# Expert weights of a mixture-of-experts kernel: GpSimd issues the next expert's staged loads itself

## The reference

```python
logits = (xt @ w_router) + b_router            # 256 tokens, 32 experts
top_v, top_i = lax.top_k(logits, 4)
gates = jax.nn.softmax(top_v, axis=-1)
# for the rows xb of each expert e:
hdn = xb @ w_gate_up[e] + b_gate_up[e]         # 1024 x 2048 weights
y = clamped_swiglu(hdn) @ w_down[e] + b_down[e]  # 1024 x 1024 weights
out = out.at[tok].add(y * gate)
```

## Time and profile before

| | |
|---|---|
| median of 3 runs | 2048.03 us (2046.79 to 2048.07) |
| profiled execution | 2044.31 us |
| its span | 2042.5 us |
| granted TensorE clock, mean | 0.982 |
| TensorE busy | 1941.8 us (95%) |
| GpSimd busy | 580.8 us (28%) |
| experts, first block to last | about 221 to 1179 us of the span |

### The profile page before, as it was taken

One profiled execution on the slowest core, in us unless ns is written; L12 is line 12 of the kernel. 1 busy time (PEld: TensorE's weight loads), 2 busy tenths in 40 slices (PEclk: granted clock), 3 DMA queues, 4 the chain that ended last, 5 costly groups with the idle time before them and its releaser, 6 DMA issues.

```text
span 2042.5 us, 28146 instructions
## 1 busy us (share of the span) xinstructions
PE 1941.8 (95%) x10641; PEld 1197.4 (59%) x10642; DVE 897.4 (44%) x1387; ACT 719.5 (35%) x1182; POOL 580.8 (28%) x622
## 2 busy tenths in 40 slices
PE   5997899999999999999999989999999999999998
PEld 2975333333333333333333379788888898898887
DVE  4644321121222112211122166658787575576983
ACT  2544111111111111111111156655665456646662
POOL 3230344442432444344433304000232030001340
PEclk7998899999999999999999989999999999999999
DMA  9999799998997999899999955445455454554553
GB/s 345 299 367 370 311 422 422 422 422 367 404 423 313 423 422 422 356 420 422 422 422 422 417 185 199 130 159 188 159 188 206 151 199 132 166 198 133 186 194 116
DMA packets 186533, 608.81 MB, mean 298 GB/s; under 512 B 10459, under 2 KB 115055, under 8 KB 133489
## 3 DMA queue, kind: packets, MB, share of 16 engines
q1 hardware_dynamic: 180976, 585.14, 74.4%
q0 software_dynamic: 5152, 21.67, 3.0%
q10 hardware_dynamic: 328, 0.95, 0.1%
HBM read 606.65 MB, written 9.26 MB: 302 GB/s over the span
## 4 chain that ended last, share of the span: by engine, by line
PE 73%; DMA 15%; DVE 6%; ACT 3%; issue 2%; SPq 1%; POOL 0%; ACTq 0%; DVEq 0%
PE bank L922 21%; PE bank L1284 16%; PE bank L959 10%; PE bank L1309 9%; DMA ring<-in_w_down 7%; PE bank L961 5%; DMA side<-in_w_gate_up 3%; DMA ring<-in_w_gate_up 3%; PE bank L1235 2%; DVE split L1770 1%; PE bank L1248 1%; PE bank L1276 1%; DMA consts<-in_w_gate_up 1%; DMA ring<-in_w_ada 1%; PE bank L1050 1%
## 5 line engine op out<-in xcount | busy, mean ns | idle before, releaser
L1284 PE MATMUL bank<-ring,qkv 128*64 128x512 f32 x2240 | 493.3, 595 | 14.9 <-DMA ring<-in_w_gate_up 10.8
L1284 PEld LDWEIGHTS bank<-ring,qkv 128*64 128x64 f32 x2240 | 155.6, 137 | 334.3 <-issue 297.8
L1770 DVE TENSOR_TENSOR split<-ring,split 128x2048 fp32r<-128x2048 f32 x104 | 250.5, 2409 | 115.2 <-ACT split L2198 115.1
L959 PE MATMUL bank<-hT_both,split 128*128 128x512 f32 x800 | 282.7, 398 | 7.0 <-DVE split L1770 7.0
L1309 PE MATMUL bank<-ring,qkv 128*64 128x512 f32 x1120 | 251.9, 597 | 5.8 <-DMA ring<-in_w_down 5.3
L2198 ACT ACTIVATE split<-ring 128x2048 fp32r<-128x2048 f32 x104 | 199.1, 1915 | 130.7 <-PE bank L922 126.1
L961 PE MATMUL bank<-hT_both,split 128*128 128x256 f32 x800 | 224.1, 280 | 0.0
L1744 DVE TENSOR_SCALAR qkv<-bank 128x512 f32<-128x512 f32 x35 | 24.2, 692 | 407.7 <-PE bank L1284 407.7
L1758 DVE SCALAR_TENSOR_TENSOR out_halves<-bank,small,out_halves 64x512 fp32r<-64x512 f32 x70 | 52.5, 750 | 342.1 <-ACT out_halves L2181 341.6
L2170 ACT ACTIVATE qkv<-qkv 128x512 f32<-128x512 f32 x35 | 22.1, 631 | 504.4 <-DVE qkv L1744 504.4
L959 PEld LDWEIGHTS bank<-hT_both,split 128*128 128x128 f32 x800 | 150.2, 188 | 45.0 <-DVE split L1770 8.3
(11 more groups left out here) (365 smaller groups left out, 3105.5 us busy)
## 6 DMA issues: line engine op xcount, KB each, us to landing
ring<-in_w_down SPq DMA_DIRECT2D x150, 1024.0 KB, 16.8
ring<-in_w_gate_up SPq DMA_DIRECT2D x70, 1024.0 KB, 17.8
probs<-in_w_gate_up SPq DMA_DIRECT2D x62, 1024.0 KB, 18.2
ring<-in_w_in SPq DMA_DIRECT2D x58, 1024.0 KB, 5.4
ring<-in_w_up SPq DMA_DIRECT2D x44, 1024.0 KB, 5.1
qkv<-in_w_gate_up SPq DMA_DIRECT2D x31, 1024.0 KB, 21.4
consts<-in_w_gate_up SPq DMA_DIRECT2D x31, 1024.0 KB, 20.4
side<-in_w_gate_up SPq DMA_DIRECT2D x31, 1024.0 KB, 23.3
```

What stands on the lines that cost most here:

```text
L959: pe.matmul(b[:, :].rearrange("p (h t) -> p h t", h=2), w_high[:, k, rows], hT_both[:, :, k, :], start=(k == 0), stop=False, skip_group_ch ...
L1284: last = pe.matmul(hidden[q][CAP * j:CAP * j + CAP, :], xgT[:, k % 4, k // 4, :], unit_at(k)[:, c:c + 512], start=False, stop=(k == KC - 1 ...
L1770: dve.tensor_tensor(low, unit_at(u % RING_L), high.bitcast(F32), ALU.subtract).then_inc(low_done, 1)
```

## The change

GpSimd itself issues the load of the next expert's staged unit, on its own DMA queue, right after the copy that empties the staging buffer; it waits for the end of that copy first. Its loop body becomes a helper, `staged_copies`, called for the first expert, in a loop for experts 2 to 30, and for the last, where nothing follows. The staged units of experts 2 to 31 count on semaphores of their own (`landed_again`). The sync engine keeps the staged units of expert 1, which it loads before the loop, and in the loop issues the direct units alone; the special order from expert 28 on is gone.

```diff
--- before.py
+++ after.py
@@ -39,7 +39,6 @@
 HALVES = 2
 MOE_UNITS = 12
 STAGED = 6
-AHEAD_UNTIL = 28
 EXPERTS, TOPK = 32, 4
 CAP = 64
 BLOCKS = EXPERTS + T * TOPK // (CAP + 1)
@@ -606,7 +605,7 @@
         landed = [sem(f"landed{s}") for s in range(RING + 4)]
         first_order, first_slot, first_turn, first_held = first_slots()
         landed_moe = [sem(f"landed_moe{s}") for s in range(MOE_UNITS)]
-        landed_staged = [sem(f"landed_staged{s}") for s in range(STAGED)]
+        landed_staged, landed_again = ([sem(f"{n}{s}") for s in range(STAGED)] for n in ("landed_staged", "landed_again"))
         bands_in, pick_ready = sem("bands_in"), sem("pick_ready")
         landed_l = [sem(f"landed_l{s}") for s in range(RING_L)]
         high_done, low_done, hT_high = (sem(n) for n in ("high_done", "low_done", "hT_high"))
@@ -761,12 +760,6 @@
                     sp.wait_ge(moe_used[u], before)
                     load_unit(e, u)
 
-            def load_ahead(e, units):
-
-                for u in units:
-                    sp.wait_ge(landed_moe[u], e + 15)
-                    load_staged(e, u)
-
 
             sp.wait_ge(*full("bturn7"))
             for u in (0, 1):
@@ -792,17 +785,7 @@
             sp.wait_ge(*full("logits4"))
             load_staged(1, 2)
             sp.wait_ge(*emptied("list"))
-            with sp.Fori(1, AHEAD_UNTIL) as e:
-                before = blocks_before(e)
-                following = sp.snap(e + 1)
-                load_ahead(following, (0, 1, 2))
-                load_direct(e, before, (6, 7))
-                load_ahead(following, (3,))
-                load_direct(e, before, (8, 9, 10, 11))
-                load_ahead(following, (4, 5))
-            load_direct(AHEAD_UNTIL, blocks_before(AHEAD_UNTIL), range(STAGED, MOE_UNITS))
-            with sp.Fori(AHEAD_UNTIL + 1, EXPERTS) as e:
-                load_ahead(e, range(STAGED))
+            with sp.Fori(1, EXPERTS) as e:
                 load_direct(e, blocks_before(e), range(STAGED, MOE_UNITS))
 
             n_blocks = sp.value_load(lists[0:1, BLOCKS + EXPERTS:BLOCKS + EXPERTS + 1], min_val=EXPERTS, max_val=BLOCKS)
@@ -2441,19 +2424,27 @@
             pool.wait_ge(bias_ready, 1)
             pick_rows(slice(0, 4))
             pool.wait_ge(*emptied("list"))
-            with pool.Fori(1, EXPERTS) as e:
+            def staged_copies(e, asked_for, landings, following):
+
                 blocks_before = pool.value_load(lists[0:1, bass.ds(BLOCKS + e, 1)], min_val=1, max_val=BLOCKS)
-                landings = pool.snap(16 * e)
                 pool.wait_ge(moe_used[0], blocks_before)
                 pool.tensor_tensor(passed[:, STAGED:], zeros[:, 0:1], zeros[:, 0:1], ALU.add)
                 pick_rows(bass.ds(4 * e, 4))
                 for u in range(STAGED):
                     pool.wait_ge(landed_moe[u], 16)
-                    pool.wait_ge(landed_staged[u], landings)
+                    pool.wait_ge(asked_for[u], landings)
                     pool.wait_ge(moe_used[u], blocks_before)
                     pool.tensor_tensor(passed[:, u:u + 1], zeros[:, 0:1], zeros[:, 0:1], ALU.add)
                     pool.tensor_copy(unit_at(u), staged_at[u]).then_inc(landed_moe[u], 1)
-                pool.wait_ge(landed_moe[STAGED - 1], e + 16)
+                    pool.wait_ge(landed_moe[u], e + 16)
+                    if following is not None:
+                        rows = w_gate_up[0, bass.ds(following, 1)].rearrange("e (k p) n -> (e p) k n", p=P)
+                        pool.dma_start(staged_at[u], rows[:, u, :]).then_inc(landed_again[u], 16)
+
+            staged_copies(1, landed_staged, 16, 2)
+            with pool.Fori(2, EXPERTS - 1) as e:
+                staged_copies(e, landed_again, pool.snap(16 * e - 16), pool.snap(e + 1))
+            staged_copies(EXPERTS - 1, landed_again, 16 * (EXPERTS - 2), None)
             pool.wait_ge(landed_moe[STAGED - 1], 16 + EXPERTS - 1)
             pool.dma_start(bdown, b_down[0]).then_inc(bdown_in, 16)
             pool.dma_start(const("bands"), shape_table[:, bands_from:bands_from + bands_n]).then_inc(bands_in, 16)
```

## The result

| | before | after |
|---|---|---|
| median | 2048.05 us (4 runs, 2046.79 to 2049.35) | 2070.57 us (4 runs, 2065.52 to 2075.29) |
| ratio | | 1.0113, 95% interval 1.0095 to 1.0131 |
| profiled execution, span | 2044.31, 2042.5 | 2068.62, 2067.0 |
| granted clock, mean | 0.982 | 0.973 |
| experts, from the first block's bias to the end of the last block | 221.5 to 1178.7 | 221.2 to 1200.9 |

Slower by 1.1%, 4.9 us under the predicted 2075.5. The profiled execution grew by 24.3 us, against the sum's 27.5; 22.6 of them are inside the experts, where the change is.

A forecast was written before the change was run, and what follows sets the result against it. Transfers bound the experts: 29.82 us per expert against a 26.45 us TensorE block, once the buffers' lead is gone. 5.0 + 5.0 + 8.7 + 8.8 = +27.5 us takes 2044.31 to 2071.8; with 3.7 for the median, 2075.5 us, range 2055 to 2100.

The forecast's parts named there:

- the sum: All terms on the profiled execution: 5.0 + 5.0 + 8.7 + 8.8 = +27.5 us.
- Half of the engines: In the experts, GpSimd's always busy queue takes half the DMA rate; TensorE waits for w_down from a stretch's third or fourth block.
- the rival of no change: Experts: the buffers' lead absorbs the mix of queues, only cheap restarts of 3.0 us stay; 2051 us or less, chance 0.09.
- First and second stretch: Spans between two-block experts, ending near 500 and 850 us: last w_down lands two units later, +5.0 us each.
- Restarts: Three starts of DMA-bound stretches (225, 635, 850 us): GpSimd's wait, latency and slower loop cost 2.9 us each, +8.7 us.
- the "faster" rival: After gaps, early requests for units 3 to 5 fill idle DMA time, up to 11.4 us over three restarts; 2037 us, chance 0.08.
- The end: Last block starts when expert 30's last w_down unit lands and takes a full 26.45 us, outlasting the last byte: +8.8 us.
- Beyond the experts: After 1179 us: nothing else on the path moves, since what follows waits for the last block; no term.
- Staged units over half: Staged units run ahead by a whole further expert, 4 units more, +19.7 us over three stretches; 2095 us, chance 0.20.
- The direct queue keeping its lead: GpSimd gets slightly under half, direct units land in time, only the end's +8.8 us is paid; 2057 us, chance 0.13.

The follow-up runs named there:

- gp_three: The changed kernel, but GpSimd asks only for staged units 0 to 2, the sync engine for 3 to 5 at their old places; 2063.59 us, 1.0070 of before.
- sp_early: The kernel before, on one queue, with staged unit 3 asked for ahead of units 6 and 7, and 4 and 5 ahead of w_down; 2050.76 us, ratio 1.0017.
- gp_slow: The changed kernel, with the last quarter of each staged copy made by a slower addition of zeros; 2070.03 us, 1.0117 of before.
- gp_tail: The changed kernel, but the sync engine again asks for the staged units of experts 29 to 31 in the old order; 2058.47 us, 1.0049 of before.
- sp_table_late: The kernel before, with GpSimd's 1024 KB table load held until the last expert's last w_down unit has landed; 2046.95 us, ratio 0.9984.

## Why the prediction was right, and where it was off

**Half of the engines.** Right, and exact. The queues of after in 300 to 490 us (packets, MB, share):

```profile
DMA packets 11011, 80.16 MB, mean 422 GB/s; under 512 B 1226, under 2 KB 1226, under 8 KB 1226
...
q1 hardware_dynamic: 5509, 40.11, 50.7%
q0 software_dynamic: 5502, 40.05, 50.7%
```

40.11 and 40.05 MB, and together 422 GB/s, as one queue had. Six staged units at half rate last longer than a block, so GpSimd's queue always has work. The landing times of w_down units asked for in 245:275 and 404:440 us, as in the earlier trace rows:

```profile
DMA to landing us min/median/max: 9.6/12.3/18.9
...
DMA to landing us min/median/max: 21.3/25.3/27.7
```

9.6 to 18.9 us where it was 4.8 to 10.6 at once after the start. The first late unit is the one that lands at 328.47 us, at the end of the fourth block (27.7 us instead of 26.45), as worked out. The Trainium skill, "DMA: Bandwidth & Descriptors" (Queues, rings and completion order), says that each engine serves its queues in turn, packet by packet; the trace agrees, with 5509 and 5502 packets. Its other rule, which stood as the rival of no change (Issuing engines are not separate DMA queues), holds for the bytes a second, 422 GB/s in both kernels, and misses the time: what the second queue takes away here is the priority of one request over another.

**First and second stretch.** Predicted 5.0 us each for two units in front of the last w_down unit, plus a restart. Measured 8.1 and 4.8. In all stretches the last wait is one block earlier than I thought, for w_down of the expert before the one whose wait I had taken. In the first that unit landed at 477.70, before the change at 467.92: 9.8 us later, four units, because all six staged units of the next expert and two of the expert after next (472.12 and 477.08) were in, where four had been. The block behind it then runs without a wait and gives 3.37 back. By the terms of the prediction that is 5.0 + (2 x 2.485 - 3.37) = 6.6 us. The other 1.6 are the clock: the eight matmuls took 2.96 instead of 1.94 us and the bias 1.71 instead of 1.12. Together 8.2, measured 8.1. gp_three repeats this bill with three units and no fall of the clock: 4.3 worked out, 4.3 measured. In the second stretch the last waited landing (833.47) has seven staged units in front of it and an eighth about half through (it lands at 836.05), where four had been: 3.5 x 2.485 - 3.37 = 5.3 us by the same terms, measured 4.8.

**Restarts.** Wrong: this term, 8.7 us, was mis-sized, and no loss of that kind is left in the trace. The wait (0.66 us) and the loop (3.3 us) were as predicted; the latency was not, as a GpSimd load on idle engines lands 5.1 us after its request and one of the sync engine after 4.8, 0.3 us more where I took 1.6. And I charged the parts as if the DMA engines carried them through the stretch. The second stretch began 8.9 us later (first landings 651.47, before 642.54: 8.1 of shift and 0.8 of restart), and all 18 buffers were full at 859.36, before at 852.01: 7.4 us later. In the first stretch they were full 0.7 us earlier than before (501.90 and 502.64), and the last unit of the third landed 12.4 us later (1189.11 and 1176.68), 0.4 less than the shift of 12.9 with which that stretch began. So the loss at each restart was made up, most likely by the early requests for units 3 to 5 that the "faster" rival names, as in sp_early. gp_slow fits: 3.4 us more in each loop of six copies left the median where it was and cost some 3 us in the profile.

**The end.** Predicted 8.8, measured 9.4 for the stretch. The mechanism is the one told, with one step off: I let the last block wait for w_down of expert 30, but the last wait is for that of expert 29 (1144.67), and both blocks behind it run through. The last weight unit is in at 1189.11, while TensorE still has 11.8 us of work; some 1.4 us of the 9.4 are the lower clock in the x8 matmuls (3.31 instead of 1.94). gp_tail takes back 9.3 of them. The stage ended at 1200.9 and not at 1206.

**The sum.** That 27.5 came near 24.3 is in part luck. The three stretches were put too low, 18.8 us against 22.3, mostly by the lower clock after waits, which the sum did not have; the restarts were put 8.7 us too high; and 2.2 us outside the experts stood at nothing.

**Beyond the experts** I put nothing, and 2.2 us were added there. In the profiles of these kernels that part is 0.6 us (gp_slow) to 4.9 us (sp_table_late) longer than in before, in no order with the change; the cause stays open.

**The rivals.** Staged units over half: the share is exactly half, and yet the run-ahead that it names occurs, by two units in the first stretch (1.6 us) and one to two in the second, where it had four in each of three. The direct queue keeping its lead: no, the lead is gone after the fourth block. Faster: its gap is real, its direct units do not come first.

## What to carry to other kernels

When the DMA engines were full, a second queue added no bandwidth (422 GB/s with one and with two), and took away an order: each busy queue got half, whatever was needed first. That it would be the same with a second queue of another engine than GpSimd was not tried. Before splitting a queue, ask for each unit how long its window is from request to use; here direct units had 24.7 us and staged ones 38 to 46, and the equal share made the short window the late one. Look at the end of such a stage by itself, and ask whether the last byte or the last full block sets it: here about half of the loss (12.1 of 22.5 us in the medians, 9.3 of 22.3 in the traces) came back with the requests of three experts, and one table load moved behind the last weights gave the only version faster than before, by 0.16%.

## What was not expected of the hardware

**The clock fell after most waits of about 3 us.** Before, TensorE's matmuls waited often but for at most 1.4 us at a time (weight loads 2.3), and the window from 230 to 1160 us has full speed (2.4 GHz) all through:

```profile
230.00:1160.00 930.00, 908.69 (x4100) 321.70 (x4096) 188.38 (x306) 130.12 (x206) 382.11 (x427) 1.00 0.99 407
```

In after, matmuls wait up to 3.0 us (weight loads 3.9), and these windows stand around two such waits:

```profile
410.00:420.00 10.00, 6.97 (x30) 2.05 (x28) 0.00 (x0) 0.10 (x1) 2.58 (x3) 0.85 1.01 422
420.00:430.00 10.00, 10.00 (x39) 3.45 (x38) 1.92 (x4) 1.36 (x2) 3.52 (x7) 0.80 1.02 423
470.00:480.00 10.00, 6.96 (x30) 1.79 (x26) 0.00 (x0) 0.00 (x0) 2.29 (x2) 0.93 1.01 422
480.00:490.00 10.00, 10.00 (x42) 3.80 (x42) 1.92 (x4) 1.37 (x2) 0.00 (x0) 0.90 1.02 423
```

The granted clock is 0.80 to 0.93 in them, a mean over stretches at 2.4 and at 1.2 GHz; at its lowest, in 800 to 810 us, it was 0.66. Nine waits of 3.0 us stand in the experts of after. Behind seven of them the eight matmuls took 2.72 to 3.70 us; behind the other two (773.84 and 995.59) they took 1.94, as at full speed. gp_three, too, has a wait of 3.0 us with no fall of the clock:

```profile
470.00:480.00 10.00, 6.96 (x32) 2.13 (x30) 0.72 (x1) 1.37 (x2) 1.04 (x2) 1.00 1.01 421
```

So a wait for a transfer of 3 us cost up to 1.8 us more than itself in the matmuls right behind it, but not each time; what decides is not shown. My sum did not have this item. Where the next wait was for bytes anyway, the slower matmuls only shortened it.

**Issues took longer on the fuller queue.** Before, the sync engine's DMA issue took 0.33 us after a gap, and 1.985 to 1.991 us for `side` at 446.9 and 475.4, late in the stretch, with single ones up to 3.9 us. In after, where a unit on that queue waits as long but each moves at half the rate, so that about half as many stand in it, every issue of the sync engine in the experts takes 0.33 us. In the chain of waits of before two such issues do stand (3.75 us at 423.10 and 1.96 at 427.07), but the engines moved 422 GB/s from 415 to 450 us, so no bytes came later by them. That the depth of the queue is the cause is argued, not tested.

**The first block of the experts** took 28.6 us in some executions and 31.4 to 31.6 in others, of the order on one queue and of GpSimd's alike, with its first matmuls at a lower clock (granted clock 0.50 in 215 to 225 us of gp_slow, 0.77 in before). A shift of 3 us between two single profiles here can be that; the stretches above are counted from block 1 on where kernels differed in it.
